# Start addresses of the operands of one-pass products, moved to multiples of 128 bytes

## What is computed

```
def hybrid_layer(x, ...):
    h = rms_norm(x, norm_g[0])
    proj = h @ w_in
    ...
    gates = jax.nn.sigmoid(merge_logit.reshape(B_, S_, N_BRANCH, D_))
    merged = (gates[:, :, 0] * (y_a @ w_branch[0])
              + gates[:, :, 1] * (y_b @ w_branch[1])
              + gates[:, :, 2] * (y_c @ w_branch[2]))
    x = x + rms_norm(merged @ w_out, norm_g[1])
    h = rms_norm(x, norm_g[2])
    gt, up = jnp.split(h @ w_ffn_in, 2, axis=-1)
    x = x + rms_norm((jax.nn.silu(gt) * up) @ w_ffn_out, norm_g[3])
...
for i in range(DEPTH_2):
    mix = _ssd_mixer(x, ...) if i % 2 == 0 else _dilated_attention_mixer(x, ...)
    x = _layer_norm(DEEPNORM_ALPHA * x + mix, ...)
    x = _layer_norm(DEEPNORM_ALPHA * x + _hierarchical_moe(x, ...), ...)
```

## The kernel before

| buffer, stage | begins at (bytes) | past a multiple of 128 |
|---|---|---|
| `hT` hi and lo, all stages | 51840, 68224 | 0 |
| `ahead`, slot 0 of all `project` and `gated` stages | 221152 | 96 |
| `cut` of the recurrence's input projection (27 to 121 us) | 156384 | 96 |
| `cut` of the recurrent unit's projection (121 to 212) | 193408 | 0 |
| `cut` of the NSA queries (212 to 258) | 156288 | 0 |
| `cut` of GLA q and k (477 to 522), GLA v (527 to 620) | 190080, 196224 | 0 |
| `cut` and `branch` of the merge (667 to 942) | 189056, 156288 | 0 |
| `cut` of the output projection (944 to 991) | 195296 | 96 |
| `cut` of the FFN input (1007 to 1252) | 176768 | 0 |
| `cut` of the FFN output (1254 to 1378) | 193248 | 96 |
| `cut` of the SSD input (1391 to 1527) | 170912 | 32 |
| `cut` of SSD z (1528 to 1623) | 177056 | 32 |
| `cut` of the SSD output (1783 to 1875) | 179296 | 96 |
| `cut` of attention q, k, v (2471 to 2677) | 188064 | 32 |
| `cut` and `oT` of the attention output (2779 to 2796) | 117376, 173696 | 0 |
| `scan_wall`, `scan_one` | 212608, 213120 | 0 |

## Time and profile before

### The profile page before, as it was taken

The page is one execution under the profiler, slowest core; times in us unless marked ns, Lnnn a source line. Parts: engine busy times, 40 slices in busy tenths (PEclk is TensorE's granted clock), DMA queues, the critical chain, the costliest instruction groups (busy, mean ns, idle before and its releaser), DMA issues. The chain is left out here.

```text
span 3389.3 us, 41253 instructions
## 1 busy us (share of the span) xinstructions
PE 3007.8 (89%) x15935; PEld 2130.9 (63%) x15935; DVE 1155.7 (34%) x1831; ACT 851.3 (25%) x1731; POOL 468.5 (14%) x662
## 2 busy tenths in 40 slices
PE   7998989899989999999899897888689898887875
PEld 6787769778768878789777533333278775333332
DVE  3553754323453333427364400000263463000002
ACT  2514841332223320114460111111111241111111
POOL 0031520000000000000260111111122321111111
PEclk9998999999989999999799898898789998989897
DMA  3242022134333323222004599999733126999996
GB/s 127 87 105 76 2 75 79 36 87 99 93 91 89 99 81 99 87 87 75 3 19 164 233 391 399 387 408 397 302 111 103 41 96 266 399 396 391 394 406 259
DMA packets 250299, 604.73 MB, mean 178 GB/s; under 512 B 39646, under 2 KB 203868, under 8 KB 225468
## 3 DMA queue, kind: packets, MB, share of 16 engines
q1 hardware_dynamic: 238268, 583.05, 47.4%
q0 software_dynamic: 10560, 16.27, 1.4%
q10 hardware_dynamic: 1344, 3.67, 0.5%
HBM read 595.56 MB, written 24.16 MB: 183 GB/s over the span
## 5 line engine op out<-in xcount | busy, mean ns | idle before, releaser
L2872 PE MATMUL bank<-slot,moe_xT 128*64 128x512 f32 x1856 | 492.7, 691 | 145.2 <-DMA slot<-in_moe_w_up 139.5
L2872 PEld LDWEIGHTS bank<-slot,moe_xT 128*64 128x64 f32 x1856 | 167.9, 159 | 428.5 <-issue 419.4
L2966 DVE TENSOR_TENSOR ex_h<-ex_gate,bank 64x512 f32<-64x512 f32 x64 | 44.2, 690 | 929.7 <-ACT ex_gate L2929 929.6
L248 PE MATMUL bank<-hT_hi,cut_lo 128*128 128x512 f32 x1248 | 312.9, 393 | 0.0
L248 PE MATMUL bank<-hT_hi,ahead 128*128 128x512 f32 x624 | 258.3, 414 | 28.7 <-DVEq L421 18.7
L248 PEld LDWEIGHTS bank<-hT_hi,cut_lo 128*128 128x128 f32 x1248 | 234.5, 188 | 53.2
L248 PE MATMUL bank<-hT_lo,ahead 128*128 128x512 f32 x624 | 256.2, 411 | 0.0
L248 PE MATMUL bank<-hT_hi,cut_hi 128*128 128x512 f32 x624 | 244.9, 392 | 1.1 <-DVE cut_hi L277 1.1
L248 PE MATMUL bank<-hT_lo,cut_hi 128*128 128x512 f32 x624 | 244.6, 392 | 0.0
L2889 PE MATMUL bank<-slot,ex_hT 128*64 128x512 f32 x960 | 217.4, 592 | 2.3 <-ACT ex_hT L2933 2.3
L2929 ACT ACTIVATE ex_gate<-bank 64x512 f32<-64x512 f32 x64 | 37.7, 590 | 621.7 <-PE bank L2872 621.6
(11 more groups left out here) (576 smaller groups left out, 5388.6 us busy)
## 6 DMA issues: line engine op xcount, KB each, us to landing
slot<-in_moe_w_gate SPq DMA_DIRECT2D x60, 2048.0 KB, 14.3
slot<-in_moe_w_up SPq DMA_DIRECT2D x60, 2048.0 KB, 18.8
slot<-in_moe_w_down SPq DMA_DIRECT2D x60, 2048.0 KB, 10.1
raw<-in_w_in SPq DMA_DIRECT2D x26, 1024.0 KB, 5.4
raw<-in_w_ffn_in SPq DMA_DIRECT2D x44, 512.0 KB, 5.0
raw<-in_ssd_w_in SPq DMA_DIRECT2D x20, 1024.0 KB, 5.3
raw<-in_attn_w_qkv SPq DMA_DIRECT2D x18, 1024.0 KB, 5.0
raw<-in_w_in SPq DMA_DIRECT2D x24, 512.0 KB, 4.3
```

The costliest lines, as they stand in the source:

```text
L248: last = nc.tensor.matmul(out, a(pa, k), b(pb, k), start=(late == "hi" and k == 0 and n == 0), stop=(late == "lo" and k == kt - 1 and n == ...
L2872: last = nc.tensor.matmul(GU[s][rows, :], xT[:, s, k * ER:(k + 1) * ER], raw[slot][which][:, k * HID:(k + 1) * HID], start=(k == 0), stop= ...
L2966: nc.vector.tensor_tensor(h[:, s, :], gate[:, s, :], GU[s][right, :], ALU.mult).then_inc(h_ready, 1)
```

## The change

`aligned` puts a filler tensor ahead of a buffer where the stack stands off a multiple of 128; `Pair`, `Cut` and the SSD scan's two float32r tensors use it. `ahead` is moved down to a multiple of 128, and the router's weights with it, since they are placed below it. `cut` of the attention output is placed at a fixed address and isn't touched. After it every buffer of the table begins at a multiple of 128. Instructions, their order and the semaphores are the same.

```
+LINE = 128
+def aligned(mem, nc, name, shape, dtype):
+    short = -((nc.sbuf_base + 31) // 32 * 32) % LINE
+    if short:
+        mem.enter_context(nc.sbuf_tensor(f"short_{nc.next_id()}", [P, short // 4], F32))
+    return mem.enter_context(nc.sbuf_tensor(name, shape, dtype))
 class Pair:
-        self.hi, self.lo = (mem.enter_context(nc.sbuf_tensor(f"{name}_{part}", shape, F32R)) for part in ("hi", "lo"))
+        self.hi, self.lo = (aligned(mem, nc, f"{name}_{part}", shape, F32R) for part in ("hi", "lo"))
 class Cut:
-        sb = lambda part, dims: mem.enter_context(nc.sbuf_tensor(f"cut_{nc.next_id()}_{part}", dims, F32R))
+        sb = lambda part, dims: aligned(mem, nc, f"cut_{nc.next_id()}_{part}", dims, F32R)
 class Router:
-        first = nc.sbuf_top - 8 * KD * P - 3 * 4 * words
+        first = K.ahead_at - 3 * 4 * words
 def ssd_scan(...):
-        wall, one = (mem.enter_context(nc.sbuf_tensor(f"scan_{n}", [P, P], F32R)) for n in ("wall", "one"))
+        wall, one = (aligned(mem, nc, f"scan_{n}", [P, P], F32R) for n in ("wall", "one"))
 def program(...):
-    K.ahead = nc.alloc_sbuf_tensor_at("ahead", [P, 2 * KD * P], F32R, offset=nc.sbuf_top - 8 * KD * P)
+    K.ahead_at = (nc.sbuf_top - 8 * KD * P) // LINE * LINE
+    K.ahead = nc.alloc_sbuf_tensor_at("ahead", [P, 2 * KD * P], F32R, offset=K.ahead_at)
```

## The result

The changed kernel took 3374.59 us as the median of 4 runs (3368.29 to 3378.73), against 3400.66 of 4 runs of the kernel before beside them (3391.30 to 3409.61): a ratio of 0.9918, 95% interval 0.9893 to 0.9943. Run again, it took 3379.80 (7 runs) against 3403.77, ratio 0.9939 (0.9917 to 0.9960). Over all executions of the study the means are 3401.4 us before (80 executions) and 3377.0 after (11): 24 us less, where 22.4 were forecast. One execution of the kernel before took 4918.85 us at a granted clock of 0.551 and is left out of every mean and ratio. The executions come from several chips, on each of which the kernel before took 3400 to 3404 us in the mean, so the chip doesn't make the difference. The size is nearly that of the forecast. What it is made of is not.

The account below looks back on a forecast made before the run. TensorE's matmul spacing was taken to bound the split-product stages, DMA the expert stretch. Terms of 17.9 + 8.1 - 3.2 - 0.4 = 22.4 us off 3404.7 gave 3382.3 us, with an 8-in-10 range of 3373 to 3396.

Parts of the forecast that it names:

- The bound: Split-product stages: TensorE is busy 98 to 100% of the window, so the matmuls' start-to-start spacing is the time.
- Term 1: 512-column stages with every weight buffer off a multiple of 128: alignment brings spacing to 226.7 ns, 17.9 us gained.
- Term 2: 512-column stages where only ahead is off: 29 periods of 96 matmuls at 0.28 us each, 8.1 us gained.
- Term 3: 256-column matmuls in the SSD z stage and attention v: aligned operands are slower, -3.2 us.
- Term 4: Matmuls just after a wait, in some dozen stages, don't run at steady spacing: 0.4 us not counted as gained.
- what stays: VectorE's roundings, small products and scan tensors: no cost or gain in splits, under 0.3 us either way in small products.
- The rival of the shared phase: Split products: only operands with equal remainders modulo 256 run fast; 13.2 us gained, 3391.5 us; chance 0.13.
- Nothing changes: Rival for the slow buffers: they are slow for where they lie, so the time stays 3404.7 us; chance 0.07.
- the expert stretches as the test: DMA-bound expert stages: the prediction is wrong if they grow or shrink by more than 5 us.

Follow-up runs that it names:

- all160: Changed kernel with every Pair, Cut and ahead starting 160 past a multiple of 256, none at a multiple of 128; 3381.22 us in one run.
- before_fed: Kernel before plus 26 useless 512-column matmuls in TensorE's waits ahead of and at the start of the SSD scan; 3407.64 us (12 runs), ratio 1.0008.
- after_fed: Changed kernel plus 26 useless 512-column matmuls in the waits ahead of and at the start of the SSD scan; 3382.54 us (9 runs), ratio 0.9946.
- same256_fed: same256 plus 26 useless 512-column matmuls in the waits ahead of and at the start of the SSD scan; 3387.89 us (6 runs), ratio 0.9944.
- same256: Changed kernel with every Pair, Cut and ahead starting 128 past a multiple of 256, where hT lies; 3376.29 us (6 runs), ratio to before 0.9925.

## Why the prediction was right and where it was wrong

**The bound** held: TensorE's spacing is the time in the split-product stages. Where it fell to 226.7 ns, whole stages shrank by as much (merge 3.0 of 3.4 forecast, FFN input 2.7 of 3.1, SSD output 2.7 of 2.5).

**Term 1 (17.9 us) failed.** Its step was "offset 32 or 96, moving or stationary: one price", so alignment to 128 is the cause. The fast pairs of the rows had both operands 128 past a multiple of 256, and what made them fast was d = 0. After the change d is 128 in the first projection, the output projection, FFN output, SSD input and attention, and 232.3 to 233.3 ns remained there, where 226.7 had been forecast. By stages: first projection 1.0 us of 3.0, output projection -0.1 of 1.3, FFN output 0.0 of 3.5, SSD input 1.4 of 3.8, attention 0.9 of 2.4 (net of its v jobs). Only SSD output came whole. `all160` shows it from the other side: nothing aligned, everything at 226.7.

**Term 2 (8.1 us)** was right in its mechanism: `ahead` against `hT` went from d = 160 to d = 0, 226.8 ns in all runs with `ahead`. It gave 5.7 us in merge and FFN input of 6.4. The six periods of the small projections (1.7 forecast) gave none that can be seen, -0.3 us: these stages are short, and their ends move by 0.6 us with the clock.

**Term 3 (-3.2 us)** had the right sign. With d = 128 a matmul costs 118.6 to 118.8 ns and not the 120.0 of d = 0, so SSD z lost 0.5 us of the 1.8 put on it.

**Term 4 and what stays** held. VectorE's busy time is 1155.1 us against 1155.7, the waits for its queue 24.2 against 24.9, those for expert weights 130.5 against 139.5.

**The rival of the shared phase** (chance 0.13) described the spacing: it listed the stages that would stay above 232 ns, all of them did, and it gave 13.2 us where the stages sum to 10.3 and, in the second profile, 12.4. It had been held down by the argument that offsets 32 and 96 cost the same. They do, because the price is all but flat (232.3 to 234.4) at six of the eight values of d; only 0 and 64 stand apart, and the kernel before had no 64 at 512 columns. A flat price for two offsets couldn't tell the two theories apart, and it was read as if it did.

**"Nothing changes"** fell. The rule beside it, from the Trainium skill (SBUF — State Buffer, Specifications) says that the memory is read in 16-byte lines; by it starts at multiples of 32 are all alike, and the table of d disagrees by up to 7.5 ns of 227. In `all160` it holds for each operand by itself: a shift common to both costs nothing.

**The missing step.** The sum went from spacing to span with nothing between, because no wait was found that could take the gain. The clock was read as a fixed property of the kernel ("near full speed in almost every slice"), when the SSD scan ran at 0.83 and could swing. From kernel to kernel that scan takes 122 to 144 us for identical work, a wider swing than the spacing was worth. A hint lay in the sum itself: it put the 15.4 us between span and median down to the start and end of a launch, but every profiled execution here took only 1.8 to 3.0 us more than its span. The other 13 us were the distance of a quick execution from the median. The text also named the expert stretches as the test: they grew by 3.4 us and 1.5, under the 5 it allowed.

So the forecast of 22.4 us met the 24 by two errors of like size: 22.4 us of spacing were 10 to 12, and the other 12 to 14 came from where there was no term, 8 to 10 of them with the clock. That the total agreed is luck. By the phase rival's own mechanism with nothing else the time would have been some 3391. The right prediction would have given the phase rival most of the chance and widened its range by 10 us to either side for the scan.

**What stays open.** Why the clock's low stretch in the scan is 17 us in one kernel and 51 in another isn't settled. Shown is that a delay of 4.5 us just ahead of it lengthened it (17 to 51 us), that 12 us some 400 us earlier shortened it in two kernels and left it as it was in a third, and that filling the waits ahead of it doesn't reliably shorten it (14 us in `before_fed`, 68 in `after_fed`, 58 in `same256_fed`). Why the operands' starts matter by their difference isn't settled either; the runs show the prices alone. `before_fed` and `after_fed` also show that one profile doesn't stand for the median: their profiled executions had the shortest and the longest scan.

## What to carry to other kernels

Compare the start addresses of the two operands of a product with each other, not with a power of two: here equal remainders modulo 256 gave 226.7 ns at 512 float32r columns, most other pairs 232 to 234 (64 apart 228.9), while at 256 columns equal remainders were the slower choice (120.0 against 116.7). When the gain is below one per cent and any stage runs at a clock under full, add a copy of both kernels with a known delay ahead of that stage, since the clock can give or take more than the edit. And two theories that agree on every row of before need a row that splits them, or chances that are nearly equal.

## What the runs showed of the hardware

- The start-to-start time of a float32r matmul with a weight load for each depends on d, the difference of the operands' starts modulo 256: 226.7 ns at d = 0, 228.9 at 64, 234.2 at 160 (512 columns), whether the weights move or stand. At 128 it is 232.3 with stationary and 233.3 with moving weights. It doesn't depend on where the pair lies: remainders of 128 and of 160 for both give the same 226.7.
- At 256 columns d = 0 is among the slowest: 120.0, against 116.7 to 118.0 at 32 and 118.6 to 118.8 at 128.
- TensorE can stand at its lower level (1.2 GHz) for 51 us, and once 68 us, of a stretch in which it is busy for 92% of the time (127.54 of 138.09 us in `same256`), and for 17 us of the same work in another kernel. Profiled again without an edit, the scan repeats within 1.5 us.
- 12.0 us of added full-clock matmuls cost -2, 2 and 17 us in three kernels that differ in addresses alone.
